# Index scores in four PSUM banks of their own, two between the steps of the query projection; half of the last tile's selection inside the pair attention's loop

## What is computed

```python
def dsa_mixer(q, ckv, k_rope, q_idx, k_idx, w_idx, w_uk, w_uv):      # "latent"
    n_keep = min(TOPK_MAX, s // 4)                                   # 128
    ...
        rel = jax.nn.relu(jnp.einsum('bqhd,bsd->bqhs', qi, k_idx))   # 8 index heads of 64
        score = jnp.einsum('bqhs,bqh->bqs', rel, wi).astype(jnp.float32)
        score = jnp.where(causal[None], score, -jnp.inf)
        _, idx = lax.top_k(score, n_keep)
        ...
        logits = (einsum('bqhr,bqkr->bqhk', qa, c_sel) + einsum('bqhe,bqke->bqhk', qr, kr_sel)) * scale
        p = masked_softmax(logits, valid[:, :, None, :])
        return jnp.einsum('bqhr,...', p, c_sel)

def fox_mixer(q, k, v, f_logit):
    cum = lax.cumsum(jax.nn.log_sigmoid(f_logit), axis=1)
        ...
        logits = einsum('bqhd,bshd->bhqs', qb, k) * scale + cum_q[..., None] - cum_k[:, :, None, :]
        p = masked_softmax(logits, causal[None, None])
        return jnp.einsum('bhqs,bshd->bqhd', p, v)
```

## Time and profile before

| | us |
|---|---|
| three runs: median (lowest to highest) | 2144.38 (2137.56 to 2146.41) |
| the profiled execution | 2140.78 |
| its span, first to last instruction | 2139.0 |
| PE busy | 1937.7 (91%) |
| VectorE, ScalarE, GpSimd busy | 754.4, 708.8, 687.9 |
| granted clock of PE, mean share of full speed | 0.954 |

### The profile page before, as it was taken

How to read it: one execution, slowest core, us unless ns; L and a number is a source line. 1 busy time by engine, 2 the same in 40 slices (tenths; PEclk the granted TensorE clock), 3 DMA queues, 4 the chain that set the end, 5 groups by cost and what they waited for, 6 DMA issues and landing times.

```text
span 2139.0 us, 27214 instructions
## 1 busy us (share of the span) xinstructions
PE 1937.7 (91%) x10953; PEld 1497.6 (70%) x10953; DVE 754.4 (35%) x1737; ACT 708.8 (33%) x1307; POOL 687.9 (32%) x395
## 2 busy tenths in 40 slices
PE   7998998587886799988999999999889999999998
PEld 6877878532322594455888888888867797888886
DVE  2161344511111523954232222232466713322223
ACT  5123541301111423155432232242266724322222
POOL 2343213011110230035434444442045533444442
PEclk9999999789898797999999999999989999999999
DMA  6232103669996521110222222211500022232210
GB/s 221 79 118 79 40 1 138 255 263 419 414 407 278 202 80 40 39 40 5 76 97 100 91 107 79 102 59 60 119 1 2 2 80 79 79 109 89 103 55 40
DMA packets 82319, 248.44 MB, mean 116 GB/s; under 512 B 12259, under 2 KB 15523, under 8 KB 69904
## 3 DMA queue, kind: packets, MB, share of 16 engines
q1 hardware_dynamic: 75936, 231.54, 29.2%
q0 software_dynamic: 4880, 9.89, 1.3%
q10 hardware_dynamic: 1376, 5.25, 0.6%
HBM read 241.89 MB, written 12.58 MB: 119 GB/s over the span
## 4 chain that ended last, share of the span: by engine, by line
PE 82%; DVE 9%; issue 4%; ACT 3%; DMA 1%; POOL 1%; ACTq 0%; DVEq 0%; POOLq 0%; SPq 0%
PE psA L1269 54%; PE psS L1540 6%; PE psA L1520 3%; PE psA L1141 2%; PE psA L1151 2%; PE psO L1717 2%; DVE big L2786 1%; PE psT L1754 1%; DVE small L2784 1%; PE psA L1624 1%; PE psA L1452 1%; ACT tok L1786 1%; PE psO L1329 1%; PE psT L1361 1%; PE psS L1745 1%
## 5 line engine op out<-in xcount | busy, mean ns | idle before, releaser
L985 POOL TENSOR_TENSOR w_lo<-ring,w_hi 128x2048 fp32r<-128x2048 f32 (+2 forms) x43 | 195.0, 4535 | 282.5 <-ACT w_hi L1786 282.5
L2258 DVE TENSOR_TENSOR x<-psA,x 128x512 f32<-128x512 f32 (+1 forms) x176 | 108.8, 619 | 323.6 <-PE psA L1269 320.5
L1786 ACT ACTIVATE w_hi<-ring 128x2048 fp32r<-128x2048 f32 (+2 forms) x65 | 117.5, 1808 | 236.6 <-PE psA L1269 236.6
L1269 PE MATMUL psA<-w_hi,hid_hi 128*128 128x512 f32 x512 | 178.5, 389 | 0.0
L1269 PE MATMUL psA<-w_lo,hid_hi 128*128 128x512 f32 x512 | 178.4, 389 | 0.0
L1269 PE MATMUL psA<-hT_hi,w_hi 128*128 128x512 f32 x504 | 176.6, 389 | 0.0
L1269 PE MATMUL psA<-hT_hi,w_lo 128*128 128x512 f32 x488 | 171.7, 389 | 0.0
L1786 ACT ACTIVATE big<-psA 128x512 f32<-128x512 f32 (+8 forms) x157 | 68.6, 460 | 299.9 <-PE psA L1269 150.4
L2258 DVE TENSOR_TENSOR scr<-scr 128x512 f32<-128x512 f32 (+2 forms) x69 | 62.2, 904 | 275.1 <-ACT hid_hi L1786 275.0
L1269 PE MATMUL psA<-w_hi,hid_lo 128*128 128x512 f32 x384 | 149.4, 389 | 0.0
L1786 ACT ACTIVATE scr<-scr,stat 128x384 f32<-128x384 f32 (+3 forms) x224 | 124.4, 556 | 70.2 <-DVE stat L2947 39.0
(11 more groups left out here) (345 smaller groups left out, 4566.3 us busy)
## 6 DMA issues: line engine op xcount, KB each, us to landing
ring<-in_mlp_w SPq DMA_DIRECT2D x32, 2048.0 KB, 8.2
ring<-in_w_in SPq DMA_DIRECT2D x8, 2048.0 KB, 8.0
ring<-in_w_gate_e SPq DMA_DIRECT2D x14, 1024.0 KB, 11.0
ring<-in_w_up_e SPq DMA_DIRECT2D x14, 1024.0 KB, 14.0
ring<-in_w_down_e SPq DMA_DIRECT2D x13, 1024.0 KB, 11.4
big<-in_w_down_e SPq DMA_DIRECT2D x12, 1024.0 KB, 17.3
ring<-in_ab_w_in SPq DMA_DIRECT2D x5, 2048.0 KB, 7.5
scr<-in_w_down_e SPq DMA_DIRECT2D x7, 1024.0 KB, 13.8
```

Source lines behind the costliest of these rows:

```text
L985: nc.gpsimd.tensor_tensor(part(w_lo, c), raw_piece(c), part(w_hi, c).bitcast(F32), ALU.subtract)\
L1269: ins = pe.matmul(o, a, b, start=(at == 1), stop=(at == 3 * len(terms)))
L1786: return nc.scalar.activation(o, i, f, **kw)
L2258: return nc.vector.tensor_tensor(o, a, b, op)
```

## The change

The index scores are no longer jobs: they have the four banks psS and psT, which nothing else uses at that time, and two semaphores of their own. Score c waits only for ScalarE's copy of score c - 4. Four scores are issued ahead of the query projection, and two after each of its first ten products (of 32). In VectorE's part, tile 3 keeps 16 of its 32 selection steps ahead of the pair attention; the other 16 stand in its loop, one after the mask of each even item from 2 to 32.

```diff
-               ("turn_qi", 4), ("forget", 1), ("index", 8 * (NT - 1)), ("bq", 4), ("turn_aq", 4), ("bk", 4),
+               ("turn_qi", 4), ("forget", 1), ("bq", 4), ("turn_aq", 4), ("bk", 4),
...
+        n_index = 8 * (NT - 1)
+
+        def index_bank(c):
+
+            return (psS + psT)[c % 4]
...
-            def feature_major(first, name, some=range(4)):
+            def feature_major(first, name, some=range(4), between=None):
...
-                    ins.then_inc(proj_ready, 1)
+                        if k == KD - 1:
+                            ins.then_inc(proj_ready, 1)
+                        if between:
+                            between(KD * m + k)
...
-            for t in range(1, NT):
-                for h in range(8):
-                    n, r = JOBS["index"] + 8 * (t - 1) + h, 64 * (h % 2)
-                    pe.matmul(begin(n)[:, 0:(t + 1) * P], qiT[r:r + 64, h // 2, t * P:(t + 1) * P],
-                              kiT[r:r + 64, 0:(t + 1) * P], start=True, stop=True).then_inc(proj_ready, 1)
-            feature_major(JOBS["bq"], "bq")
+
+            def index_pair(c0):
+
+                for c in (c0, c0 + 1):
+                    t, h, r = c // 8 + 1, c % 8, 64 * (c % 2)
+                    if c >= 4:
+                        pe.wait_ge(relu_ready, c - 3)
+                    pe.matmul(index_bank(c)[:, 0:(t + 1) * P], qiT[r:r + 64, h // 2, t * P:(t + 1) * P],
+                              kiT[r:r + 64, 0:(t + 1) * P], start=True, stop=True).then_inc(index_scored, 1)
+
+            def index_scores(step):
+
+                if step < n_index // 2 - 2:
+                    index_pair(2 * step + 4)
+
+            for c in (0, 2):
+                index_pair(c)
+            feature_major(JOBS["bq"], "bq", between=index_scores)
...
-                evac(JOBS["index"] + c, S[c % 2][:, 0:n], n, ACT.Relu)
+                act.wait_ge(index_scored, c + 1)
+                A(S[c % 2][:, 0:n], index_bank(c)[:, 0:n], ACT.Relu).then_inc(relu_ready, 1)
...
-                copied(dve, JOBS["index"] + c)
+                dve.wait_ge(relu_ready, c + 1)
...
             for t in range(1, NT):
-                for n in range(KEEP // 4):
+                for n in range(KEEP // 4 if t < NT - 1 else KEEP // 8):
                     take(t, n)
...
+                    if i % 2 == 0 and 2 <= i < 2 + KEEP // 4:
+                        take(NT - 1, KEEP // 8 + i // 2 - 1)
```

More of the change, by code:

```diff
@@ L543, in build @@
         relu_used = sem("relu_used")
+        index_scored = sem("index_scored")
+        relu_ready = sem("relu_ready")
         gate_ready = sem("gate_ready")
@@ L2104, in _ @@
             A(ncum[0:8, :], bank(n)[0:8, :], ACT.Copy).then_inc(forget_hi, 1)
-            for c in range(8 * (NT - 1)):
+            for c in range(n_index):
                 if c >= 2:
@@ L2776, in _ @@
                     .then_inc(relu_used, 1)
-            dve.wait_ge(relu_used, 8 * (NT - 1))
+            dve.wait_ge(relu_used, n_index)
             top8 = small[:, 288:296]
```

## The result

The change runs in **2124.91 us** (median of 5 runs, 2123.76 to 2131.4); the kernel before has 2144.09 (5 runs, 2136.78 to 2146.41). The ratio is 0.9937, interval 0.9917 to 0.9957: 13.4 us faster (9.2 to 17.8). A second comparison with more runs gave 0.9942 (0.9920 to 0.9963). The forecast was 2123 in a range of 2117 to 2135. The profiled execution took 2124.1 us, its span is 2122.3; in the profiles the difference is 16.7 us.

What follows compares the result with a forecast made beforehand. PE was 82% of the chain that ended last and DVE 9%, with DVE opening the pair loop. Terms: 18.3 + 1.3 - 0.6 = 19.0 us; 2142.3 - 19.0 = 2123 us, range 2117 to 2135.

Steps and rivals of the forecast that it cites:

- stage: First index score to first product of the output projection behind the pair loop; the whole forecast gain of 19.0 us.
- scores and PE's way to the loop: Index scores and projections on PE: PE reaches the pair loop at 897.8 instead of 914.17, 16.3 us earlier.
- who opens the loop: Start of the pair loop: PE and DVE level, where DVE opened it before.
- first mask: DVE's first mask of the pair loop starts at 898.6 instead of 916.90, 18.3 us earlier.
- no half clock at the loop's start: Start of the pair loop: masks not late, so PE goes on without a gap; 1.3 us gained, bounds 0 and 3.
- 16 steps in the loop: Selection steps in DVE's idle time ahead of copies out of psT: 0.6 us lost, between 0 and 1.4.
- The form change into 64-row products: Scores between query projection products: the way into 64-row form estimated at 0.10 us per pair.
- PE sets the pace of the scores: Scores between projection steps: PE never waits for a bank; margin 0.3 us per step at the least.
- The rival that scores do not overlap with large products: Scores between projection products: 24 cost 21.8 us instead of 11.3; gain 8.5, time 2134; chance 0.09.
- The rival that the loop pays for the steps: Pair loop: all 12.2 us of steps and 0.5 come back; gain 6.9, time 2135; chance 0.09, in full or by half.
- The slower rival: Projections: clock falls and stays at 1.2 GHz; 18.6 us slower, 2161 us; chance 0.03.
- The median: Whole kernel: 19.0 us off the 2142.3 mean of all four earlier runs gives 2123 us.

Runs made afterwards that it cites:

- the faster one: Pair loop of the change with the mask of an odd item ahead of the copy out of psT on VectorE: 2114.63 us, ratio 0.9873.
- whole-tile run: Against the change: all 32 selection steps of the last tile in the pair loop, two after each even item from 2 to 32; 2131.34 us.
- banks-only run: Against the change: all 24 scores, in their four banks, ahead of the query projection instead of between its products; 2127.88 us.
- the run with the fours: Against the change: four scores after every second product of the query projection instead of two after each; 2126.43 us.
- mask-first run: Against the change: VectorE's mask of an odd item ahead of the copy out of psT in the pair loop; 2114.63 us, ratio 0.9873.

## Why the prediction was right, point by point
The sign, the mechanism and the time (2123 against 2124.91) came out. That the time came so close is partly luck: the gain by the ratio is 13.4 us (9.2 to 17.8), the forecast one was 19.0 in a range of 15 to 22, and the base of 2142.3 under it was 1.8 us below the median of the five runs. What bears out the mechanism is the stage, 18.0 against 19.0, and its terms:

| term | forecast | measured |
|---|---|---|
| scores and PE's way to the loop | 16.3 earlier, arrival 70.1 after the first score | 15.75, at 70.76 |
| who opens the loop | PE and VectorE level | level (899.96 and 900.08) |
| first mask | 18.3 earlier | 17.6 |
| no half clock at the loop's start | 1.3 | 1.0 (scores of items 8 and 9: 94.55 us after the first score before, 76.00 after, 18.55) |
| 16 steps in the loop | 0.6 lost, between 0 and 1.4 | 0.5 (18.55 to 18.02): 0.35 in the second round, 0.05 to 0.07 in each later one |
| stage | 19.0 | 18.0 |

- *The form change into 64-row products* was the estimate that missed: I took 0.10 us per pair and it is 0.19, from 831.18 to 832.24 is 1.06 us for a product of 0.87. Ten times 0.09 is 0.9 us. The first four scores gave 0.3 back, since two pairs in a row take 0.54 us each and not 0.63.
- *PE sets the pace of the scores*: right. VectorE is idle for about 0.5 us ahead of each of the last pairs of accumulates (0.51 in the row shown), and PE has no wait at all.
- *The rival that scores do not overlap with large products* falls: two scores of 512 columns cost 1.06 + 0.19, not 2.24. The draining of which the Trainium skill speaks ("TensorEngine Tiling (Array Packing)", Key Properties) is no more than these 0.3 us for the way in and out.
- *The rival that the loop pays for the steps* falls for 16 of them: they cost 0.5 us of the 12.2 in this loop and 1.1 in the faster one. At 32 steps it is true in part: the further 16 cost 6.8 us.
- *The slower rival* did not come. The clock stayed at 1.00 through the scores. But the lower clock showed in the experiments that made PE wait: after standing 12 us, and after waits of 0.9, 0.6 and 1.6 us in a row.
- *The median*: 19.0 off the mean of the runs was the right size by the medians, while the ratio gives 13.4 at the middle of its interval. The forecast had no term for this. Of the 5.6 us between the two, 1.0 is the stage and 1.3 are in the profiles outside it; the rest was not found.
- The missed chance lay in the text itself: it said that PE's only waits in the loop are for masks, and used that only for a rival. (It holds for the rounds of the fox mixer; those of the latent one also have a wait of 0.24 us for ScalarE.) Acting on it was worth 8.3 us.

## What to carry to other kernels
Where two engines reach a meeting point together, shortening one of them brings little (4.3 and 0.9 us here); look for the pair of edits that shortens both (18.0). Work that waits for nobody can be put into another engine's idle time nearly for free as long as the order behind it has slack (16 steps of 0.76 us for 0.5 us here), but look at which instruction of that engine is asked for next: an item that others wait for belongs ahead of one that itself waits (8.3 us for turning two around). When PE's products are small, give them banks enough that it never has to wait, since here the clock fell behind its waits too (0.59 and then 0.50 in the index stage before, 1.00 throughout with the change). Four banks alone did not keep it up: with all scores in one row it fell once, to 0.67 over 5.2 us.

## What the runs showed of the hardware that was not expected
- Scores of 64 rows between products of 128 rows: PE takes 0.19 us more ahead of a pair (1.06 us for a product of 0.87), and pairs of 384 columns take 0.85 us when a product follows directly, 0.75 us in groups of two pairs, the last of them too.
- The granted clock fell without any long idle time: in the whole-tile run after waits of 0.88, 0.64 and 1.60 us with PE busy 0.90 of 2.50 us, and in the banks-only run with PE busy 3.71 of 4.00 us in the stretch before (0.67 in the next 5.2 us). It came back there while the scores went on (1.00 in the next 6.5 us); before the change it did not (0.50 from 836 to 855). PE's records leave no idle time in either stretch, so what makes the difference is not shown.
- The same waits did not always bring the same clock: with PE busy 2.16 of 4.00 us in the last stretch of the loop, it stayed at 1.00 behind that in the kernel before (996 to 1000) and fell to 0.65 in the run with the fours (974 to 978).
- The same step on VectorE (max, or match and replace over 512 columns) costs 0.76 us from step to step in the chain ahead of the loop (913.40 to 914.92 for two) and no more in the loop with GpSimd working beside it (mask-first run: 0.72 from the max step at 923.32 to the mask at 924.04, GpSimd busy from 922.90 to 923.99).
